# Group norm of the RWKV-7 layer: tile by tile on four engines, with the first output slab prepared inside the recurrence

## What is computed

```
y = wkv7_scan(r, decay, k, v, -kk, kk * a)
mu_y = jnp.mean(y, -1, keepdims=True)
var_y = jnp.mean(jnp.square(y - mu_y), -1, keepdims=True)
y = ((y - mu_y) * lax.rsqrt(var_y + GN_EPS)).reshape(B, L, D)
y = y * lnx_g.astype(jnp.float32) + lnx_b.astype(jnp.float32)
bonus = jnp.sum(r * k * r_k.astype(jnp.float32), -1, keepdims=True) * v
y = (y + bonus.reshape(B, L, D)).astype(x.dtype)
return (y * g) @ w_o
```

## Time and profile before

| | |
|---|---|
| median of 3 runs | 1736.08 us (1732.81, 1736.08, 1736.42) |
| the profiled execution | 1734.36 us, of which the span from the first to the last instruction is 1732.6 us |
| PE busy | 1634.2 us, 94% of the span |
| DVE, ACT, POOL busy | 1289.9, 999.6, 92.8 us |
| mean granted TensorE clock | 0.962 |
| recurrence | from 484 to 628 us of the span |
| group norm to the start of the second output slab | from 628 to 673 us |
| experts | from 735 to 1698 us |

### The profile page before, as it was taken

One profiled execution on the slowest core, in us unless ns is written; L12 is line 12 of the kernel. 1 busy time (PEld: TensorE's weight loads), 2 busy tenths in 40 slices (PEclk: granted clock), 3 DMA queues, 4 the chain that ended last, 5 costly groups with the idle time before them and its releaser, 6 DMA issues.

```text
span 1732.6 us, 29765 instructions
## 1 busy us (share of the span) xinstructions
PE 1634.2 (94%) x12050; PEld 1288.7 (74%) x12050; DVE 1289.9 (74%) x1260; ACT 999.6 (58%) x1037; POOL 92.8 (5%) x125
## 2 busy tenths in 40 slices
PE   7998999979999977799999999999999999999995
PEld 5787999949889967677777777776777777777774
DVE  3755554466744444789899898998998998998984
ACT  3645443336512221577777777777777777777773
POOL 3310000000023400000000000000000000000000
PEclk9988999989899987799999999999999999999997
DMA  9432454513300002179999999999999999999980
GB/s 260 179 122 99 175 182 185 200 49 119 126 3 4 4 26 76 55 298 369 371 359 366 371 360 371 361 367 369 359 371 373 354 369 369 361 370 360 370 315 26
DMA packets 60291, 425.40 MB, mean 246 GB/s; under 512 B 6887, under 2 KB 8023, under 8 KB 9224
## 3 DMA queue, kind: packets, MB, share of 16 engines
q1 hardware_dynamic: 58152, 416.52, 63.3%
q0 software_dynamic: 2016, 7.13, 1.6%
HBM read 422.28 MB, written 1.12 MB: 244 GB/s over the span
## 4 chain that ended last, share of the span: by engine, by line
PE 71%; DVE 3%; ACT 2%; issue 1%; ACTq 0%; DVEq 0%
PE PS L530 54%; PE PS L817 5%; PE PS L531 4%; PE PS L1035 1%; PE PS L836 1%; PE PS L991 1%; PE PS L845 1%; DVE arena L1396 1%; PE PS L570 1%; PE PS L1021 0%; PE PS L1022 0%; PE PS L576 0%; PE PS L808 0%; PE PS L959 0%; PE PS L802 0%
## 5 line engine op out<-in xcount | busy, mean ns | idle before, releaser
L1396 DVE TENSOR_TENSOR w_lo<-ring,w_hi 128x2048 fp32r<-128x2048 f32 x391 | 894.2, 2288 | 200.3 <-ACT w_hi L1325 88.1
L1325 ACT ACTIVATE w_hi<-ring 128x2048 fp32r<-128x2048 f32 x336 | 644.6, 1919 | 264.3 <-PE PS L530 241.7
L530 PE MATMUL PS<-w_hi,x_hi 128*96 128x512 f32 x896 | 353.9, 395 | 0.7 <-ACT x_hi L1317 0.7
L530 PE MATMUL PS<-w_hi,x_lo 128*96 128x512 f32 x896 | 352.5, 393 | 0.0
L530 PE MATMUL PS<-w_lo,x_hi 128*96 128x512 f32 x896 | 243.0, 392 | 0.0
L1096 ACT ACTIVATE w_hi<-ring 128x2048 fp32r<-128x2048 f32 x55 | 105.3, 1914 | 168.2 <-issue 89.9
L530 PEld LDWEIGHTS PS<-w_lo,x_hi 128*96 128x96 f32 x896 | 144.6, 161 | 62.1
L530 PEld LDWEIGHTS PS<-w_hi,x_lo 128*96 128x96 f32 x896 | 144.8, 162 | 58.5
L530 PEld LDWEIGHTS PS<-w_hi,x_hi 128*96 128x96 f32 x896 | 144.6, 161 | 57.9 <-ACT x_hi L1317 1.0
L530 PE MATMUL PS<-w_hi,hid_hi 128*96 128x512 f32 x448 | 176.7, 394 | 0.0
L530 PE MATMUL PS<-w_hi,hid_lo 128*96 128x512 f32 x448 | 176.0, 393 | 0.0
(11 more groups left out here) (261 smaller groups left out, 2051.8 us busy)
## 6 DMA issues: line engine op xcount, KB each, us to landing
ring<-in_slabs SPq DMA_DIRECT2D x395, 1024.0 KB, 4.9
arena<-in_lora POOLq DMA_DIRECT2D x1, 1152.0 KB, 5.4
h<-in_h SPq DMA_DIRECT2D x1, 1088.0 KB, 5.2
arena<-bias_lines POOLq DMA_DIRECT2D x1, 1056.0 KB, 19.6
arena<-bias_lines POOLq DMA_DIRECT2D x1, 1040.0 KB, 24.1
arena<-in_lora POOLq DMA_DIRECT2D x1, 1024.0 KB, 11.9
out<-h SPq DMA_DIRECT2D x1, 1024.0 KB, 4.7
arena<-in_lora POOLq DMA_DIRECT2D x1, 512.0 KB, 6.5
```

The lines of the kernel that those rows point to most:

```text
L530: return pe.matmul(out, x, w, start=start, stop=stop) if tokens_stay else \
L1325: act.activation(w_hi[:, n % 2, :], ring[:, n % SLOTS, :], ACT.Copy).then_inc(hi_set, 1)
L1396: tt = lambda o, a, b, op=ALU.mult: dve.tensor_tensor(out=o, in0=a, in1=b, op=op)
```

## The change

Four things are changed; the arithmetic is regrouped as `y_centred*g * lnx_g*rstd + (bonus + lnx_b)*g`.

- **The first slab.** ACT rounds `SL_O2` in four quarters behind the copies of levels 2 (two quarters), 3 and 4 of the last chunk; DVE splits it behind its steps of level 4. The split of `SL_O2 + 1` on DVE moves from ahead of the tile loop to behind it.
- **The gated bonus.** Behind each bonus product DVE makes four new steps `z = (z + lnx_b)*g_`. POOL makes `gated_y = r_*g_` for each centred tile, eight new steps. In the tile loop this leaves DVE three steps of a tile (scale, add, remainder) where four stood.
- **Group norm by tile.** PE signals each head-mean matmul; DVE subtracts, ACT squares and PE sums tile by tile. The spread root is signalled tile by tile too, and DVE takes its first tile when that tile is there. PE no longer waits for ACT's second half of `y` ahead of the first four tiles.
- **Order of the first slab on PE.** Its 16 weight tiles are taken in the order k, then m: both output tiles at each k.

The diff, cut to its core:

```diff
@@ gpsimd
+            for m in range(KC):
+                pool.wait_ge(gn_dve, GN_NORMED + m)
+                pool.tensor_tensor(out=gated_y[:, m, TEXT], in0=r_[:, m, TEXT], in1=g_[:, m, TEXT], op=ALU.mult)\
+                    .then_inc(gn_pool, 1)
@@ tensor, linear
+                    tiles = [(t, *divmod((n - base) * TILES + t, chunks)) for t in range(TILES)]
+                    if n == base and chunks < TILES:
+                        tiles.sort(key=lambda x: (x[2], x[1]))
...
@@ tensor
+            def group_norm():
+
+                pe.wait_ge(c_dve, len(DV))
                 for m in range(KC):
+                    pe.wait_ge(c_act, AV["y", N_CH - 1, 0, m // 4])
+                    pe.matmul(PS[:, m, TEXT], mean_head[:, :], r_[:, m, TEXT], start=True, stop=True).then_inc(gn_pe, 1)
                 for m in range(KC):
+                    pe.wait_ge(gn_act, m + 1)
                     mm = pe.matmul(PS[0:HEADS, 0, TEXT], to_head[:, m, :], sq[:, m, TEXT], start=m == 0, stop=m == KC - 1)
+                mm.then_inc(gn_pe, 1)
+                pe.wait_ge(gn_dve, GN_ROOT)
                 for m in range(KC):
+                    pe.matmul(PS[:, m, TEXT], from_head[:, m, :], rstd[0:HEADS, TEXT], start=True, stop=True)\
+                        .then_inc(gn_pe, 1)
@@ scalar
+                if part == "level" and c == N_CH - 1 and i >= 2:
+                    act.wait_ge(c_pe, PT["s", N_CH - 2, 0, 1])
+                    for j in ((), (), (0, 1), (2,), (3,))[i]:
+                        round_quarter(SL_O2, j)
             assert kept == len(AV)
-            act.wait_ge(c_dve, len(DV))
-            act.wait_ge(c_pe, len(PT))
-            round_slab(SL_O2)
-            act.wait_ge(gn_dve, 1)
-            act.activation(sq[:, :, TEXT], r_[:, :, TEXT], ACT.Square).then_inc(gn_act, 1)
-            act.wait_ge(gn_dve, 2)
+            for m in range(KC):
+                act.wait_ge(gn_dve, GN_NORMED + m)
+                act.activation(sq[:, m, TEXT], r_[:, m, TEXT], ACT.Square).then_inc(gn_act, 1)
+            act.wait_ge(gn_dve, GN_SUM)
@@ vector
+            def gated_bonus(i):
+
+                dve.wait_ge(c_dve, DV["bonus", N_CH - 1, i, 0])
+                for m in range(4 * i, 4 * i + 4):
+                    gn.mark(dve.scalar_tensor_tensor(out=z[:, m, TEXT], in0=z[:, m, TEXT], scalar=v_of("lnx_b", m),
+                                                     in1=g_[:, m, TEXT], op0=ALU.add, op1=ALU.mult))
...
+                    if c == N_CH - 1 and i == len(levels_of(c)) - 1:
+                        dve.wait_ge(c_pe, PT["u", c, i, 1])
+                        split_slab(SL_O2)
...
+            for m in range(KC):
+                dve.wait_ge(gn_pe, m + 1)
+                gn.mark(tt(r_[:, m, TEXT], r_[:, m, TEXT], PS[:, m, TEXT], ALU.subtract))
...
+            def scale(k):
+                dve.wait_ge(gn_pool, k + 1)
+                dve.wait_ge(gn_pe, KC + 2 + k)
+                gn.mark(dve.scalar_tensor_tensor(out=r_[:, k, TEXT], in0=gated_y[:, k, TEXT], scalar=v_of("lnx_g", k),
+                                                 in1=PS[:, k, TEXT], op0=ALU.mult, op1=ALU.mult))
...
+            scale(0)
+            for k in range(KC):
+                if k + 1 < KC:
+                    scale(k + 1)
+                dve.wait_ge(gn_dve, gn_scaled(k))
+                gn.mark(tt(r_[:, k, TEXT], r_[:, k, TEXT], z[:, k, TEXT], ALU.add))
+                assert gn.n == gn_out(k)
+                if k:
+                    split_output(k - 1)
+            split_output(KC - 1)
             split_slab(SL_O2 + 1)
```

More of the change, by code:

```diff
@@ L149, with gn_scaled, gn_out @@
 RT_SEL, RT_EXP, RT_POS, RT_FLAG, RT_GATES = 7, 9, 10, 12, 18
-GN_OUT = 3
+GN_NORMED, GN_SUM, GN_ROOT = 9, 17, 18
+def gn_scaled(k):
+    return GN_ROOT + (1 if k == 0 else 2 * k)
+def gn_out(k):
+    return GN_ROOT + (2 * k + 3 if k < KC - 1 else 2 * KC)
 LN_READY = 10
@@ L549, in linear, with before @@
                 for n in range(base, base + outs * chunks // TILES):
-                    tiles = [divmod((n - base) * TILES + t, chunks) for t in range(TILES)]
-                    def before(t):
-                        m, k = tiles[t]
+                    tiles = [(t, *divmod((n - base) * TILES + t, chunks)) for t in range(TILES)]
+                    if n == base and chunks < TILES:
+                        tiles.sort(key=lambda x: (x[2], x[1]))
+                    def before(i):
+                        _, m, k = tiles[i]
                         if k == 0 and kept is not None and m + before_out >= 8:
@@ L559, in linear @@
                     products(n, n % 2, P, [(t, x_hi(k), x_lo(k), PS[:, m, cols], k == 0, k == chunks - 1)
-                                           for t, (m, k) in enumerate(tiles)], before=before)
+                                           for t, m, k in tiles], before=before)
             def layer_norm(l):
@@ L1703, in _ @@
             assert len(steps) == len(DV)
-            dve.wait_ge(c_dve, len(DV))
-            s = Steps(gn_dve)
-            y = r_[:, :, TEXT]
-            dve.wait_ge(c_pe, len(PT))
-            split_slab(SL_O2)
-            dve.wait_ge(gn_pe, 1)
-            s.step(tt(y, y, PS[:, :, TEXT], ALU.subtract))
-            dve.wait_ge(gn_pe, 2)
-            s.mark(dve.tensor_scalar(rstd[0:HEADS, TEXT], PS[0:HEADS, 0, TEXT], 1.0 / HD, GN_EPS, ALU.mult, ALU.add))
-            dve.wait_ge(gn_act, 2)
@@ L1729, in _ @@
-            dve.wait_ge(gn_dve, s.n)
-            left(out_lo[:, KC - 1, TEXT], r_[:, KC - 1, TEXT], out_hi[:, KC - 1, TEXT], out_hi_set, KC, out_split)
+            for m in range(KC):
+                dve.wait_ge(gn_pe, m + 1)
+                gn.mark(tt(r_[:, m, TEXT], r_[:, m, TEXT], PS[:, m, TEXT], ALU.subtract))
+            dve.wait_ge(gn_pe, KC + 1)
+            gn.mark(dve.tensor_scalar(rstd[0:HEADS, TEXT], PS[0:HEADS, 0, TEXT], 1.0 / HD, GN_EPS, ALU.mult, ALU.add))
+            assert gn.n == GN_SUM
```

42 lines of the change are left out of this document (13 added, 29 removed).

## The result

The changed kernel took 1712.85 us (median of 4 runs, 1712.17 to 1718.62), against 1736.25 us before (4 runs, 1732.81 to 1738.4). The ratio is 0.9874, with a 95% interval of 0.9847 to 0.9901. The profiled execution took 1712.17 us, its span is 1710.4 us, so 22.2 us less than the span of before. The forecast was 1713.5 us.

What follows compares the result with a forecast made beforehand. It took a 44.7 us chain of waits between recurrence and second output slab as the bound. From 1734.36 us it took 21.6 us to reach 1712.8, then added half of 1.7 for 1713.5 us, range 1709.5 to 1718.

Steps and rivals of the forecast that it cites:

- What bounds the kernel: Recurrence to second output slab: one line of waits through all engines, 44.7 us; PE sets the time behind it.
- The first slab: Between recurrence and subtraction: rounding and splitting leave the path, 4.7 us, of which PE's head means (3.69, parallel) stay.
- The cover: DVE in the last chunk: 1.1 us left between the moved split's end and the first bonus product.
- rival 4: Group norm: steps by tile bring nothing, only the slab's 4.7 us go, total 1730 us; chance 0.02.
- Gated bonus, means, sums, root: Behind the recurrence: gating 1.6 us per four steps, off the path; sums end at 635.5, spreading starts at 638.3.
- Tile loop: DVE's output tiles: 1.09 us a tile instead of 1.70, the loop ending at 648.3.
- Clock and PE: PE from spreading to second slab: clock low from about 640, back near 648; gain taken as 21.6 us.
- two cases of the clock: PE's first slab: gain 20.8 us with half clock rising after 3.1 us, or 22.3 at the full clock.
- term for the spreading: PE spreading the root: 6.9 us at half clock throughout, from 638.3 to 645.2.
- half of 1.7: Total time: half of the 1.7 us by which the median before exceeded the profiled execution, added to 1712.8.
- rival 1: First slab on PE: clock stays at half through the whole slab, gain 17.6 us, total 1717 us; chance 0.08.
- the forecast's own case of 20.8: First slab on PE: half clock through the spreading, rise after 3.1 us, slab ends at 652.2, gain 20.8 us.

Runs made afterwards that it cites:

- filling the stop: Changed kernel with six added matmuls on PE, results unused, while it waits for the root: stretch 22.5 us, total 1713.61 us, ratio 0.9886.
- the long step on POOL: Changed kernel with the eight tiles' remainders on POOL instead of DVE, the last taking 2.74 us: stretch 23.8 us, total 1715.53 us, ratio 0.9901.

## Why the prediction was right

**What bounds the kernel.** Right: PE sets the time behind the second slab, and the 22.1 us won there are in the span.

**The first slab.** The cover was right: 1.1 us foretold between the split and the bonus product, 1.16 measured, and nothing moved in the last chunk. The prediction said that 4.7 us left the path here "of which the head means on PE stay", and rival 4 priced this part at 4.7 us by itself. That price was wrong: alone it is worth 0.3 us, since PE's means, with the 0.57 us of waiting for ACT ahead of them, end 0.5 us before the split did. The sum did not suffer, because it was made from the new chain's start to its end, and not by adding up what was taken away.

**Gated bonus, means, sums, root.** Four gating steps took 1.67 us (1.6 foretold). The sums ended 7.2 us behind the recurrence (7.2 foretold) at the full clock with no wait ahead. The spreading started 9.9 us behind it (10.0 foretold).

**Tile loop.** Remainders 1.06 us apart (1.09 foretold), the last one ending 19.7 us behind the recurrence (20.0 foretold).

**Clock and PE.** Low from 640.82 to 647.65, foretold "from about 640, back near 648". The slab ended 22.6 us behind the recurrence; the forecast had 23.1, between 22.4 and 23.9, so the gain was 22.1 us instead of 21.6. The mechanism was right. That the number is so close is in part luck: 21.6 is the middle between two cases of the clock, 20.8 and 22.3, and the case with the low clock, which came true, gave 20.8. Its term for the spreading, 6.9 us at half clock throughout, measured 5.61, because the clock fell 1.66 us into it. In the runs in which it fell ahead of the spreading this stage took 7.19 us, near the 6.9. Last, half of 1.7 added to 1712.8 makes 1713.6, not 1713.5.

**A wrong sign.** The prediction named "PE continuously busy from the spreading to the slab's end" as the mark of rival 1, the clock staying at half. PE was so busy, and rival 1 was not true: the clock came back at 647.65, and PE took the last tile at 649.42, 0.5 us behind the end of its remainder (648.91). The sign could not have told the cases apart, since the forecast's own case of 20.8 has PE behind DVE as well. PE, slowed by the half clock, set the end, and DVE's loop was 0.5 us ahead of it. That is why no relief showed: filling the stop gave 0.1 us, a shorter DVE loop would have given nothing even without the long step on POOL, and with the clock at 1.00 throughout DVE's loop set the end and only 0.3 us were won.

**Where the 22.1 us came from.** Undone one at a time, the parts cost 3.4 (slab early), 3.3 (order), 4.4 (three steps and the gating) and 9.7 us (by tile), with the clock's part in each of them. They are not independent: the slab alone in the old kernel is worth 0.3 us. A fall of the clock ahead of the spreading makes the last remainder 1.1 us late, and these 1.1 us are in the 3.3, the 4.4 and the 9.7; half clock behind the last remainder is in the 3.4 (1.6), the 3.3 (1.1) and the 9.7 (1.9). One part was undone by no run: DVE takes the first spread tile when it is there, and no longer waits for all eight. Its first scale, before and after:

```profile
653.67 0.48 DVE L1721 SCALAR_TENSOR_TENSOR arena<-arena,vec,PS 128x256 f32<-128x256 f32 x1 [4.88 <-PE PS L808]
```

```profile
639.96 0.91 DVE L1739 SCALAR_TENSOR_TENSOR arena<-arena,vec,PS 128x256 f32<-128x256 f32 x2 [0.86 <-PE PS L819]
```

It started 7.2 us behind the start of the spreading (646.44), and now starts 0.8 us behind it (639.16). These 6.4 us are read from the rows and not shown by an experiment.

## What to carry to other kernels

Price a chain of stages from the new chain's start to its end, not as a sum of removed pieces: a step that stands in the chain of waits may have a path of nearly the same length beside it, and then its removal is worth little until that other path is shortened too. Turning whole-tensor steps into tile steps paid most here, because it took away waits of PE and with them the half clock of the stages behind. When two engines end a stage within half a microsecond of each other, relief of one of them alone wins no more than that.

## What the runs showed of the hardware

- The spreading matmuls with 16 rows of weights read as busy PE, but the clock fell or stayed low beside them. With PE filled ahead of them it fell 2.64 us into them; with the same fill and 112 rows of zeros added it never fell. After a fall ahead of them it stayed at 0.50 through all of them (6.76 us busy of 6.83 in the earlier trace rows, 7.11 of 7.64 with subtraction and square whole); with 112 rows of zeros added it was back after 3.42 us, 3.03 of them busy. Each of these is one profile.
- Behind the 16-row matmuls the full ones did not bring the clock back at once, though PE was busy without a break: it took 2.95 us of them in the changed kernel (644.70 to 647.65), 4.9 with the fill and 6.0 with subtraction and square whole (658.05 to 664.06).
- The place of the fall differs from run to run against the program, from 0.6 us ahead of the spreading's start to 2.0 us behind it in the profiles without a fill, and is worth 1.6 us in the spreading alone (5.61 against 7.19 us) and 1.1 us at DVE's last remainder.
- DVE and POOL, with both inputs of each in SBUF, slow each other. DVE's adds of 128x256 took 0.56 us instead of 0.42. POOL's remainders of 128x256 stood 0.87 us apart; its products, beside DVE steps with one input in `PS`, stood 0.69 apart, though these are not the same operation. A POOL step of 128x256 beside a DVE step of 2048 columns took 2.74 us, and the DVE step 2.82 instead of 2.29. The Trainium skill (SBUF — State Buffer, section Who interferes with whom) says that a VectorE instruction with two SBUF inputs contends with a GpSimd instruction that reads SBUF. These rows agree.
